# Eight turns of the first feed-forward with 512-column gate and up matmuls

## What is computed

```python
def swiglu_ffn(h, w_in, w_out):
    gate, up = jnp.split(h @ w_in, 2, axis=-1)
    return (jax.nn.silu(gate) * up) @ w_out

for layer in range(2):
    h = h + 0.5 * swiglu_ffn(rms_norm(h, ffn1_norm[layer]), ffn1_w_in[layer], ffn1_w_out[layer])
    h = h + mixer[layer](rms_norm(h, mix_norm[layer]))
    h = h + 0.5 * swiglu_ffn(rms_norm(h, ffn2_norm[layer]), ffn2_w_in[layer], ffn2_w_out[layer])
return rms_norm(h, final_norm)
```

## Time and profile before

| | |
|---|---|
| median of 3 runs | 1019.82 us (1016.94 to 1022.36) |
| the profiled execution, its own time | 1019.72 us |
| its span, first to last instruction | 1017.9 us |
| TensorE's granted clock, mean | 0.998 |
| PE / DVE / ACT / POOL busy | 98 / 73 / 56 / 11 per cent |
| first feed-forward | the first 219 us |

### The profile page before, as it was taken

The page is one execution under the profiler, slowest core; times in us unless marked ns, Lnnn a source line. Parts: engine busy times, 40 slices in busy tenths (PEclk is TensorE's granted clock), DMA queues, the critical chain, the costliest instruction groups (busy, mean ns, idle before and its releaser), DMA issues.

```text
span 1017.9 us, 20105 instructions
## 1 busy us (share of the span) xinstructions
PE 996.4 (98%) x7672; PEld 924.7 (91%) x7672; DVE 743.0 (73%) x906; ACT 565.7 (56%) x784; POOL 111.6 (11%) x143
## 2 busy tenths in 40 slices
PE   8999999999889999999999999999999999999997
PEld 8999998999789999999999999999899898888886
DVE  5789886989977666666687666668566577666666
ACT  7444445473255555555575555556599775555554
POOL 4863148000001000000010000001000010000000
PEclk9999999999999999999999999999999999999999
DMA  7555553443156465555546555554643245556552
GB/s 250 195 180 166 186 180 108 150 145 126 43 167 190 164 197 185 182 183 184 187 158 206 182 184 183 183 185 159 210 143 125 84 155 199 191 188 190 188 187 108
DMA packets 49037, 172.42 MB, mean 169 GB/s; under 512 B 6096, under 2 KB 6096, under 8 KB 48976
## 3 DMA queue, kind: packets, MB, share of 16 engines
q1 hardware_dynamic: 48832, 171.52, 51.6%
q10 hardware_dynamic: 144, 0.02, 0.0%
HBM read 170.47 MB, written 1.05 MB: 169 GB/s over the span
## 4 chain that ended last, share of the span: by engine, by line
PE 86%; DVE 9%; ACT 2%; issue 2%; DMA 1%; SPq 0%; DVEq 0%; ACTq 0%
PE mx L1184 11%; PE gu L1184 10%; PE gu L1168 8%; PE gu L1169 8%; PE gu L1170 8%; PE acc L1168 6%; PE acc L1169 6%; PE acc L1170 6%; PE mx L1186 6%; PE gu L1186 5%; PE acc L1212 2%; PE acc L1214 2%; PE acc L1216 2%; DVE w_lo L725 1%; DVE tmp L952 1%
## 5 line engine op out<-in xcount | busy, mean ns | idle before, releaser
L793 DVE TENSOR_TENSOR w_lo<-raw,w_hi 128x1024 fp32r<-128x1024 f32 x178 | 217.3, 1223 | 57.3 <-ACT w_hi L417 56.4
L725 DVE TENSOR_TENSOR w_lo<-raw,w_hi 128x1024 fp32r<-128x1024 f32 x138 | 178.3, 1307 | 47.2 <-ACT w_hi L332 46.8
L417 ACT ACTIVATE w_hi<-raw 128x1024 fp32r<-128x1024 f32 x171 | 179.9, 1053 | 41.2 <-PE mx L1186 19.2
L1168 PE MATMUL gu<-g,w_hi 128*128 128x256 f32 x624 | 179.7, 288 | 1.5 <-DVE w_lo L1088 1.4
L332 ACT ACTIVATE w_hi<-raw 128x1024 fp32r<-128x1024 f32 x145 | 150.6, 1051 | 49.1 <-DMA raw<-wstream_dram 23.1
L1169 PE MATMUL gu<-g,w_hi 128*128 128x256 f32 x624 | 176.5, 283 | 0.0
L1170 PE MATMUL gu<-g,w_lo 128*128 128x256 f32 x624 | 176.5, 283 | 0.0
L1184 PE MATMUL mx<-g,w_hi 128*128 128x512 f32 x480 | 170.8, 398 | 0.0
L1184 PE MATMUL gu<-g,w_hi 128*128 128x512 f32 x432 | 153.6, 398 | 0.0
L1168 PE MATMUL acc<-h_hi,w_hi 128*128 128x256 f32 x504 | 144.1, 286 | 1.7 <-DVE h_lo L747 1.6
L1169 PE MATMUL acc<-h_lo,w_hi 128*128 128x256 f32 x504 | 143.4, 284 | 0.0
(11 more groups left out here) (279 smaller groups left out, 1704.6 us busy)
## 6 DMA issues: line engine op xcount, KB each, us to landing
raw<-wstream_dram SPq DMA_DIRECT2D x318, 512.0 KB, 3.6
raw<-wstream_dram SPq DMA_DIRECT2D x4, 256.0 KB, 5.6
x<-x_in_dram SPq DMA_DIRECT2D x4, 256.0 KB, 5.8
out_dram<-x_tok SPq DMA_DIRECT2D x4, 256.0 KB, 2.0
gain_row<-last_gain_dram SPq DMA_DIRECT2D x1, 512.0 KB, 4.5
s_memory<-b_re_dram SPq DMA_DIRECT2D x1, 256.0 KB, 4.1
s_memory<-b_im_dram SPq DMA_DIRECT2D x1, 256.0 KB, 4.3
s_memory<-c_re_dram SPq DMA_DIRECT2D x1, 256.0 KB, 3.6
```

Of the source, the lines that this page charges most:

```text
L417: act.activation(w_hi[:, n0 % RING, :], raw[:, n0 % RAW, :], ACT.Copy).then_inc(hi_ready, 1)
L725: dve.tensor_tensor(lo, raw[:, n % RAW, :], hi.bitcast(F32), ALU.subtract).then_inc(lo_ready, 1)
L793: dve.tensor_tensor(w_lo[:, n0 % RING, :], raw[:, n0 % RAW, :], w_hi[:, n0 % RING, :].bitcast(F32), ALU.subtract).then_inc(lo_ready, 1)
L1168: pe.matmul(dst, a, hi, start=start, stop=False, skip_group_check=check)
```

## The change

In turns 2 to 6 and 12 to 14 of the first feed-forward the gate and up units take the wide form. ACT copies the upper halves before it rounds the unit's successor, and makes silu and h before its last rounding of the turn; DVE sums and scales in place of scaling alone. The semaphore counts of the later loops are moved by eight. PE waits for the reads of `mx` before turn 12, and for the scaling of turn 6 before it writes `mx` in turn 7 and of turn 14 before it does in turn 15.

```diff
--- before.py
+++ after.py
@@ -52,6 +52,7 @@
 UNITS = FFN_BASE[3] + FFN_UNITS
 BODY = 4
 PREP_TURNS = range(2, NF)
+PREP_WIDE = (2, 3, 4, 5, 6, 12, 13, 14)
 AHEAD = (ATT_BASE + 3 * KB + 4, ATT_BASE + 3 * KB + 5)
 TURNS = (NF - 2) // BODY
 WIDE_TURNS = BODY * TURNS - 1
@@ -495,6 +496,17 @@
 
                 g0 = gate_unit(FFN_BASE[0], f)
                 early, late = 2 * (f - FIRST_TURNED), 8 + 2 * (f - LATE_TURNED)
+                if f in PREP_WIDE:
+                    split_after(g0)
+                    act.wait_ge(unit_done, g0 + 2)
+                    act.wait_ge(hlo_ready, f - 1)
+                    act.activation(tmp[:, f % 2, 2:4, :], (mx, gu)[f % 2][:, :, SEQ:2 * SEQ],
+                                   ACT.Copy).then_inc(low_copied, 1)
+                    split_after(g0 + 1)
+                    silu(0, f)
+                    round_h(0, f)
+                    split_after(g0 + 2)
+                    return
                 if f == NF - 1:
                     read_turned(late)
                     silu(0, f)
@@ -786,7 +798,7 @@
                             scale_gu(m % 2, 3 * BODY * i + (g0 + 1))
                             hidden(m % 2, f1, 2)
                         elif k == 1 and not last_turn(m, i):
-                            sum_gu(m % 2, BODY * i + (WIDE_TURNS * (n - 1) + m + 1), f1)
+                            sum_gu(m % 2, BODY * i + (len(PREP_WIDE) + WIDE_TURNS * (n - 1) + m + 1), f1)
                         n0 = g0 + k + RING
                         if not isinstance(i, int) or n0 + 3 * BODY * i < UNITS:
                             dve.wait_ge(hi_ready, 3 * BODY * i + (n0 + 1))
@@ -889,7 +901,10 @@
                 split_after(g0)
                 if 0 <= f - FIRST_PRODUCT < 12:
                     s5_product(f - FIRST_PRODUCT)
-                scale_gu(f % 2, g0 + 2)
+                if f in PREP_WIDE:
+                    sum_gu(f % 2, PREP_WIDE.index(f) + 1, f + 1)
+                else:
+                    scale_gu(f % 2, g0 + 2)
                 if KERNEL_TURN < f <= KERNEL_TURN + 2:
                     read_kernels(f - KERNEL_TURN - 1)
                 if 0 <= f - FIRST_ROTATED < 4:
@@ -1395,8 +1410,20 @@
                 pe.wait_ge(gu_scaled, f - 1)
                 if f == NF - 1:
                     g0 -= 1
+                if f in PREP_WIDE:
+                    if f == PREP_WIDE[5]:
+                        pe.wait_ge(turned_read, 8)
+                    for r in range(2):
+                        pe.wait_ge(lo_ready, g0 + r + 1)
+                        wide_unit((mx, gu)[f % 2][:, r, :], (g0 + r) % RING)
+                    pe.wait_ge(lo_ready, g0 + 3)
+                    pe.wait_ge(hlo_ready, f)
+                    down_unit(0, (g0 + 2) % RING, (f + 1) % 2)
+                    return
                 pe.wait_ge(lo_ready, g0 + 1)
                 column_unit(gu[:, f % 2, 0:SEQ], g0 % RING)
+                if f in (FIRST_TURNED, KERNEL_TURN):
+                    pe.wait_ge(gu_scaled, f)
                 if 0 <= early < 8:
                     turn(early)
                 if 8 <= late < 16:
```

## The result

Over 20 runs each the changed kernel takes 1020.78 us in the median (1019.66 to 1025.23), the kernel before 1018.69 us (1016.54 to 1022.36): ratio 1.0021, 95% interval 1.0012 to 1.0030. It is slower by 0.2 per cent, under the 0.5 per cent set as the bound for a difference that counts here, but clear of the noise of 20 runs. The profiled execution took 1020.73 us, span 1019.0 us.

The account below looks back on a forecast made before the run. PE, busy 996.4 of 1017.9 us, was taken as the bound. Matmuls -0.9, PE waits in turns 6 and 7 +0.3, kernels waiting for product and padding +0.7 gave +0.1: 1019.8 us, no change, range 1015.6 to 1023.2.

Parts of the forecast that it names:

- PE's saving: Turns 2 to 6 and 12 to 14: wide matmuls save PE 0.11 us a turn, 0.9 us in all.
- DVE's period: Wide turns: the sum costs 0.72 us, the split gives back 0.53, so 8.07 becomes about 8.3 us, under PE's 8.53.
- The tie in turn 5: h_lo, behind POOL's padding copies, ready at 66.2 us when PE wants it at 66.1: PE waits 0 to 0.3 us.
- DVE catches up: Turns 7 to 10: PE's longer turns let DVE recover its delay, so from turn 11 it goes by PE's time.
- ACT's wait at 110.61: Turn 11: ACT waiting for PE's gate unit, taken as the sign that DVE goes by PE's time from there.
- What sets turn 15: First kernel matmuls wait for turn 14's product and POOL's last padding: 0.1 us earlier to 0.4 later, +0.7 in the sum.
- A: Rival: DVE becomes the bound, h_lo of turn 5 and last padding come late: +3.5 us, 1023.2 us; chance 0.14.
- the split's wait: DVE's third split waits 0.46 us for ACT's rounding; ACT's new order removes this, saving 0.53 us a turn.
- C: Rival: a 1.3 us pause ahead of turn 15's kernels brings 3.4 us at lower clock: +1.5, 1021.3 us; chance 0.10.
- B: Rival: the 2.5 us stall in turn 15's kernels and the lower clock behind it go: -4.0, 1015.8 us; chance 0.10.

Follow-up runs that it names:

- the run with the kernels after the up unit: The changed kernel with both halves of turn 15's S5 kernels moved behind the up unit: 1022.42 us, ratio 1.0039 to the kernel before.
- spread kernels: S5 kernels in four quarters after turn 15's gate, up, down and turn 16's gate units: kernel before 1015.61 us (0.9965), changed kernel 1019.13 us (1.0001).
- the run with the late turns alone: The changed kernel with only turns 12 to 14 wide, turns 2 to 6 left narrow: 1017.37 us, ratio 0.9992 to the kernel before.
- the control with the kernels moved: The kernel before, without wide turns, with both halves of turn 15's S5 kernels behind the up unit: 1019.25 us, ratio 1.0008.
- ACT's new order alone: The kernel before with only ACT's third rounding put ahead of the silu in turns 2 to 6 and 12 to 14: 1018.87 us, ratio 0.9992.

## Why the prediction was right or wrong

The time lay in the range and within 0.5 per cent, but no change was forecast and 0.2 per cent slower was measured. That it came within 1 us of the forecast is luck: a delay that the forecast didn't have was largely offset by a stall that it took as fixed. Step by step:

- **PE's saving** was right: 0.45 us in turns 2 to 5, 0.9 in all where nothing holds PE back. Wide pairs take 0.353 us, as the pairs of the same shape did before. Less the 0.12 us of a 256-column matmul that leaves 0.23 us for 512 columns. The trace so disagrees with the 131 ns that the Trainium skill ("TensorE: Matmul & The Clock Gate", "Back-to-back issue gap") gives as the sustained spacing at 512 columns.
- **DVE's period** was right: 8.31 us against 8.3, with the split 0.34 us behind the hidden product and no wait ahead of it.
- **The tie in turn 5** was mis-sized. I had the hidden product behind POOL's second copy, but not the scaling beside the first. It took 1.93 instead of 0.68 us and POOL's pair 0.27 us longer, h_lo was done at 67.2 instead of 66.2, and PE waited 0.92 us where I had 0 to 0.3. Of that 1.0 us of delay 0.74 is the later start of the first product: where the changed turns ran with that product at 41.27, as before (the run with the kernels after the up unit), h_lo was done at 66.45, and PE, itself 0.3 us earlier, waited 0.73 us.
- **"DVE catches up" in turns 7 to 10 is the step that failed.** I took PE's longer turns there as room, and ACT's wait at 110.61 as the sign that DVE goes by PE's time from turn 11 on. But between the products of turns 7 and 10 DVE takes the same time in both kernels (27.26 and 27.25 us), so it had no room from PE there at all. What it could absorb was waiting that its own rows show. Of the two gaps of some 0.2 us before turn 11's product the first stayed (0.18 us in both kernels) and the second went, which gave the 0.31 us. The spread kernels, with equal starts, show the change's own part: 1.76 us late in turn 7, 1.80 in turn 11, nothing absorbed. ACT's wait at 110.61 showed that ACT was early, not DVE.
- **What sets turn 15** was right in kind: padding, and before it the last product. The term was sized at +0.7 us, with the first kernel matmul at most 0.4 us later than before. It came 3.2 us later, since it inherited the delay that wasn't caught up: 2.25 us at turn 11, of which 1.8 are the wide turns'. With equal starts (the spread kernels) it came 2.7 us later.
- **The rivals.** A came true in its mechanism (DVE's delay decides, and it is paid at the padding), although the split's wait was recovered as forecast. C's pause came, with 2.6 us instead of 1.3, and the clock fell in it. B came in part: 1.7 us less stall and no lower clock in the down unit. I had them as exclusive cases; they came together, +3.2 + 1.3 - 3.2 us, and the sum looked like little change. By the Trainium skill's page "Runtime: NRT & Kernel Launch", section "Instruction fetch mechanics", as the prediction read it, the stall was to stay at its place in the stream. It did, ahead of the 308th kernel matmul, and the traces agree with that section's blocks of 256 instructions: all stalls stand at the ends of such blocks. The step that failed in B is from the place to the length: the stall shrank with the pause and went with lower density.

## What to carry to other kernels

A late engine catches up only by the waits that its own rows show; an engine with longer turns beside it gives no room if the late one wasn't waiting for it. Before a wait is priced, look at what stands behind it: here not quite half of the change's price (1.6 of 3.7 us in the medians) was paid by a shorter stall, because the burst of tiny instructions behind the pause would have stalled anyway. And a burst of some 300 tiny matmuls is worth spreading between larger ones before anything is done about matmuls that save 0.05 us a unit.

## What I had not expected of the hardware

- Dense runs of 32- and 96-column matmuls stop PE with no semaphore named, at the ends of blocks of 256 instructions: two groups of 160 behind a pause of 1.67 us run without a stall, behind one of 1.58 us they stall 1.4 us, two groups with a normal unit in between and a gap of 0.42 us ahead stall 2.5 us, 320 in a row 5.5 us with the change and 2.3 us without, four groups of 80 not at all. What is short is instructions: each stall ends 1.2 to 1.5 us after a packet of 16 KB in the instruction queue. The queues of the DMA as a whole weren't full in the longest stall, where they moved 130 GB/s. All of this is read from profiled executions; whether one without profiling stalls as long isn't shown.
- A pause of 2.6 us let the granted clock fall to the 1.2 GHz level even though PE was busy for all but 0.1 of the 78.5 us ahead of it; a pause of 1.67 us, in the run with the late turns alone, didn't. The length of the pause doesn't settle it: the clock also fell 0.5 us behind a stall of 2.03 us (the control with the kernels moved) and didn't behind one of 2.13 us (ACT's new order alone).
- Two SBUF-only operations of DVE beside POOL's copies take 1.93 and 1.48 us instead of 0.69 and 0.42, one beside each of the two copies, and POOL's pair takes 4.19 instead of 3.92 us. The scaling in the narrow form, which reads PSUM, runs beside the start of the same copy in 0.68 us.
